# Layer-norm sums of the prompt in an mLSTM block: products with ones take the place of GpSimd's additions

## What is computed

```
def _head_layernorm(x, g):
    xf = x.astype(jnp.float32)
    xc = xf - jnp.mean(xf, axis=-1, keepdims=True)
    var = jnp.mean(xc * xc, axis=-1, keepdims=True)
    return xc * lax.rsqrt(var + EPS) * g.astype(jnp.float32)
...
# in _mlstm_chunked, for every frame of a chunk:
h = num / jnp.maximum(jnp.abs(den), jnp.exp(-mj))[..., None]
C_new = wpL[..., None, None] * C + jnp.einsum('bhs,bhsv,bhsd->bhvd', wsL, vb, kb)
...
hC = _head_layernorm(hC, p['mlstm_norm'][c]).reshape(B, T, C_INNER) + p['mlstm_skip'][c].astype(f32) * xc
```

## Time and profile before

| | |
|---|---|
| time, median of 3 runs | 2273.56 us (2268.47 to 2276.02) |
| time of the profiled execution | 2260.29 us |
| its span, first to last instruction | 2258.5 us |
| TensorE's mean granted clock | 0.965 of full |
| busy: PE, PEld | 2074.6 us (92%), 1879.0 us (83%) |
| busy: DVE, ACT, POOL | 863.3 us (38%), 429.3 us (19%), 919.6 us (41%) |
| the four loops over the units, together | 241.63 us |

### The profile page before, as it was taken

The page is one execution under the profiler, slowest core; times in us unless marked ns, Lnnn a source line. Parts: engine busy times, 40 slices in busy tenths (PEclk is TensorE's granted clock), DMA queues, the critical chain, the costliest instruction groups (busy, mean ns, idle before and its releaser), DMA issues.

```text
span 2258.5 us, 33584 instructions
## 1 busy us (share of the span) xinstructions
PE 2074.6 (92%) x13453; PEld 1879.0 (83%) x13453; DVE 863.3 (38%) x1115; ACT 429.3 (19%) x670; POOL 919.6 (41%) x584
## 2 busy tenths in 40 slices
PE   6999998889999999899999787878689899999997
PEld 5999987889999999899887263535389899999996
DVE  5654556442221012679322453544422322210125
ACT  3242333121110001222123131312100211100011
POOL 4333322354444444655442031313254544444443
PEclk9999999999999999999999998989789999999998
DMA  4121221112222222232222727272722122222222
GB/s 167 54 92 57 82 89 48 58 56 75 74 74 76 77 77 75 96 121 76 104 90 74 268 86 273 92 274 84 252 108 75 56 75 74 74 75 75 75 75 93
DMA packets 81879, 224.35 MB, mean 99 GB/s; under 512 B 6288, under 2 KB 11280, under 8 KB 81040
## 3 DMA queue, kind: packets, MB, share of 16 engines
q1 hardware_dynamic: 73152, 202.94, 26.5%
q10 hardware_dynamic: 8656, 20.39, 2.5%
HBM read 170.06 MB, written 53.25 MB: 99 GB/s over the span
## 4 chain that ended last, share of the span: by engine, by line
PE 75%; DVE 13%; DMA 5%; issue 3%; ACT 3%; DVEq 1%; SPq 0%; POOL 0%; ACTq 0%; POOLq 0%
PE psd L210 10%; PE psd L214 10%; PE psd L215 10%; PE psd L211 10%; PE psd L217 10%; PE psd L216 10%; DMA Cs<-st_c 4%; DVE cv L901 2%; DVE ntmp L284 2%; PE psm L389 2%; DVE Cs L1370 1%; PE psd L1207 1%; PE psd L1196 1%; PE psm L1298 1%; DVE cv L898 1%
## 5 line engine op out<-in xcount | busy, mean ns | idle before, releaser
L1810 POOL CAST whi<-wraw 128x1024 fp32r<-128x1024 f32 x224 | 236.4, 1055 | 915.4 <-PE psd L217 500.3
L1812 POOL TENSOR_TENSOR wlo<-wraw,whi 128x1024 fp32r<-128x1024 f32 x224 | 543.2, 2425 | 18.0
L210 PE MATMUL psd<-xh,whi 128*128 128x320 f32 x1280 | 405.8, 317 | 25.3 <-ACT xh L257 14.0
L214 PE MATMUL psd<-xl,whi 128*128 128x320 f32 x1280 | 401.3, 314 | 13.9 <-POOL xl L292 10.9
L216 PE MATMUL psd<-xh,wlo 128*128 128x320 f32 x1280 | 398.2, 311 | 0.0
L217 PE MATMUL psd<-xh,wlo 128*128 128x320 f32 x1280 | 398.1, 311 | 0.0
L215 PE MATMUL psd<-xl,whi 128*128 128x320 f32 x1280 | 398.0, 311 | 0.0
L211 PE MATMUL psd<-xh,whi 128*128 128x320 f32 x1280 | 397.9, 311 | 0.0
L210 PEld LDWEIGHTS psd<-xh,whi 128*128 128x128 f32 x1280 | 243.1, 190 | 29.8 <-issue 23.4
L214 PEld LDWEIGHTS psd<-xl,whi 128*128 128x128 f32 x1280 | 242.2, 189 | 21.9 <-POOL xl L292 15.8
L211 PEld LDWEIGHTS psd<-xh,whi 128*128 128x128 f32 x1280 | 243.0, 190 | 0.8 <-issue 0.2
(11 more groups left out here) (352 smaller groups left out, 2904.5 us busy)
## 6 DMA issues: line engine op xcount, KB each, us to landing
wraw<-w SPq DMA_DIRECT2D x224, 512.0 KB, 3.3
Cs<-st_c SPq DMA_DIRECT2D x32, 1024.0 KB, 8.1
c_s<-Cs SPq DMA_DIRECT2D x32, 1024.0 KB, 5.1
z_kept<-zb ACTq DMA_DIRECT2D x16, 320.0 KB, 2.2
ztp<-z_kept SPq DMA_DIRECT2D x4, 1024.0 KB, 7.7
c_p<-Cp SPq DMA_DIRECT2D x4, 1024.0 KB, 9.9
xT<-x SPq DMA_DIRECT2D x4, 640.0 KB, 6.7
x_kept<-xT ACTq DMA_DIRECT2D x1, 2560.0 KB, 8.6
```

Source lines behind the costliest of these rows:

```text
L210: pe.matmul(o0, wh, x0, start=st, stop=False)
L214: pe.matmul(o0, wh, l0, start=False, stop=False)
L1810: pool.tensor_copy(whi[s][:], wraw[s][:]).then_inc(w_high, 1)
L1812: pool.tensor_tensor(wlo[s][:], wraw[s][:], whi[s][:].bitcast(F32), ALU.subtract).then_inc(w_split, 1)
```

## The change

POOL's seven additions per head go, and with them the semaphore `G`. In unit 2 PE multiplies each of the four tiles of `hb` with `ones` and accumulates the products in `B[0]`; in unit 6 it does so with the four squares in `kT` and with `D` in `att`. The wait for `G` in unit 2 falls away, since the wait for `dn` already covers ACT's writing of `hb`; in unit 6 a wait for the last square takes the place of the waits for `sD` and for the last centred tile.

```diff
-                self.G = Steps(sem("m_G"), [("h", k) for k in range(1, KH)] + [("s", k) for k in range(1, KH)] + ["sD"])
...
                     if u == 2:
                         pe.wait_ge(S_.sem, S_.at("dn", h))
-                        pe.wait_ge(self.G.sem, self.G.at(("h", KH - 1), h))
-                        pe.matmul(B[0], ones, kT[:, 0, 0:SEQ], start=True, stop=True).then_inc(P_.sem, 1)
+                        for k in range(KH):
+                            mm = pe.matmul(B[0], ones, hb[:, KH * h + k, 0:SEQ], start=(k == 0), stop=(k == KH - 1))
+                        mm.then_inc(P_.sem, 1)
                     if u == 6:
-                        pe.wait_ge(self.G.sem, self.G.at("sD", h))
-                        pe.wait_ge(V_.sem, V_.at(("xc", KH - 1), h))
-                        pe.matmul(B[0], ones, kT[:, 0, 0:SEQ], start=True, stop=True).then_inc(P_.sem, 1)
+                        pe.wait_ge(S_.sem, S_.at(("sq", KH - 1), h))
+                        for k in range(KH):
+                            pe.matmul(B[0], ones, kT[:, k, 0:SEQ], start=(k == 0), stop=False)
+                        pe.matmul(B[0], ones, att[:, 0:SEQ], start=False, stop=True).then_inc(P_.sem, 1)
...
             def pool_head(self, pool, h):
...
-                one = kT[:, 0, 0:SEQ]
-                for k in range(1, KH):
-                    pool.wait_ge(S_.sem, S_.at(("num", k), h))
-                    if k > 1:
-                        pool.wait_ge(G_.sem, G_.at(("h", k - 1), h))
-                    pool.tensor_tensor(one, hb[:, KH * h, 0:SEQ] if k == 1 else one, hb[:, KH * h + k, 0:SEQ], ALU.add)\
-                        .then_inc(G_.sem, 1)
-                for k in range(1, KH):
-                    pool.wait_ge(S_.sem, S_.at(("sq", k), h))
-                    if k > 1:
-                        pool.wait_ge(G_.sem, G_.at(("s", k - 1), h))
-                    pool.tensor_tensor(one, one, kT[:, k, 0:SEQ], ALU.add).then_inc(G_.sem, 1)
-                pool.wait_ge(G_.sem, G_.at(("s", KH - 1), h))
-                pool.wait_ge(S_.sem, S_.at("D", h))
-                pool.tensor_tensor(one, one, att[:, 0:SEQ], ALU.add).then_inc(G_.sem, 1)
```

More of the change, by code:

```diff
@@ L1571, in pool_head @@
             def pool_head(self, pool, h):
-                S_, G_ = self.S, self.G
                 if h == 0:
```

## The result

The changed kernel takes 2291.02 us (median of 6 runs, 2286.74 to 2293.73), the kernel before 2273.76 us (median of 6, 2268.47 to 2276.55): 17.3 us more, ratio 1.0076 with a 95% interval of 1.0059 to 1.0094. The profiled execution took 2290.63 us. The forecast was 2289.0. Two executions further on, one of e4 and one of e12, took 2654 and 2632 us at a mean granted clock of 0.74, and the medians and ratios leave them out.

A forecast was written before the change was run, and what follows sets the result against it. PE's own work and the loads of the streams' memory, not POOL, were taken to bound the loops. Unit 6's 15.4 us plus 0 for unit 2 and 0 for waits, on 2273.6, gave 2289.0 us; range 2280 to 2298.

The forecast's parts named there:

- What bounds the kernel: In the loop over units, PE and loads of the streams' memory set the pace; POOL's sums were ready 10 and 17 us sooner.
- Unit 6, 15.4 us: Four more products per head on PE's own path in unit 6, nothing hiding them: 3.84 us per head, 15.4 over four.
- The price per product: Each added fp32 128x512 product with ones in units 2 and 6 takes 0.96 us on PE, 1.9 at the lower clock.
- Unit 2, 0 us: Three more products per head in unit 2, 2.9 us on PE, hidden by load waits: 0 us.
- The cover: Idle time ahead of unit 4, 7.66 us, hides unit 2's 2.9; unit 5's load keeps at least 0.6 us to spare.
- The clock: Rival: less low clock in the loops gives back nearly all, one in 25, or 3 to 8 us, one in 9.
- The rival's mechanism: The shorter wait ahead of unit 4, 4.8 us for 7.66, could keep the clock up: 1.8 us per head in three heads.
- The sum: Unit 6's 15.4 us, plus 0 for unit 2 and 0 for the waits, makes 15.4 us over the whole kernel.
- The three rivals outside of the range: Unit 2's products showing, 0.05; the clock giving all back, 0.04; POOL's additions having held something up, 0.02.
- The 4.8 us from the sum to the normaliser: Sign of being right: in unit 6, 4.8 us between the second sum's start and the start of `nu` in each head.
- a sign of being wrong: A head longer by over 5 us, with the wait for the load ahead of unit 5.
- The idle time ahead of unit 4: Sign of being right: PE's idle time there near 4.8 us where it was 7.66, with unit 4's start unchanged.

The follow-up runs named there:

- e4: Changed kernel with the variance's five products moved from unit 6 to the end of unit 5, ahead of the load wait: 2267.19 us, ratio 0.9973 to before.
- e12: Kernel before with variance and normaliser products moved to the end of unit 5, plus unread products at the end of unit 3: 2243.55 us, ratio 0.9864.
- e3: Kernel before with POOL's additions left out, each sum being one product over the first tile alone: 2270.92 us, ratio 0.9993.
- e2: Kernel before with only unit 6's sum made by five products, POOL still adding the four tiles for unit 2: 2287.09 us, ratio 1.0055.
- e10: Changed kernel with four unread products with ones added at the end of unit 5: 2280.74 us, ratio 1.0034 to before.
- e11: Kernel before with four unread products with ones added at the end of unit 5: 2262.59 us, ratio 0.9940.
- e1: Kernel before with only unit 2's sum made by four products, POOL still adding the squares and D: 2276.52 us, ratio 1.0010.
- e8: Changed kernel with unit 2's four products made twice over: 2279.86 us, ratio 1.0030 to before.
- e7: Changed kernel with unit 6's five products made twice over: 2303.41 us, ratio 1.0129 to before.
- e9: Changed kernel run and profiled once more, nothing altered: 2295.09 us, ratio 1.0082 to before.
- e0: Kernel before profiled once more, nothing altered: 2275.48 us.

## Why the prediction was right

- *What bounds the kernel.* Right: without POOL's additions and the waits for them the time is the same within 4 us (e3), and in the loops PE or the loads end last.
- *Unit 6, 15.4 us.* The place and the mechanism were right (e2, e4). The price per product was mis-sized: a row of products with the same ones matrix takes 4.40 us for five at full clock, not 4.80. In e10:

```profile
1400.83 3.70 PE L1281 MATMUL psd<-mqk,con 128*128 128x512 f32 x8
1404.37 1.02 PE L1282 MATMUL psd<-att,con 128*128 128x512 f32 x2
1405.23 0.38 PE L1285 MATMUL psm<-att,con 128*128 128x128 f32 x2
```

  Less the 0.96 of the one product before, this is 3.44 us per head, 13.8 in all where I had 15.4. Measured in the stretch: 12.3 us between e10 and e11, 11.6 between the changed kernel and the second profile of before.
- *Unit 2, 0 us.* The cover held for PE and for the load of unit 5: unit 4 starts 31.3 us behind unit 0 in the second head, as before. It was thinner than I worked out: unit 5's load took 11.3 us before, beside unit 4's load, and not the 7.37 to 9.46 that I compared with. In the changed kernel it took 8.7 us and landed 0.3 us ahead of its use. The whole part costs 0 to 5 us (e1), not the 0 that I took. The step that fell short is the first head: I asked only whether unit 3 would be late, and it is not, but the shorter idle time moves the low clock to unit 4, and unit 6 starts some 4 us later in five of six profiles. Why its load takes 9.9 us and not 7.3 stays open.
- *The clock.* The rival's mechanism exists, as e8 shows with twice the products, but three added ones don't reach it: over both profiles of the changed kernel unit 4's read went at the low clock in five of the six heads behind the first, and at full clock in one, after 4.22 us of idle time. The idle time of 3.72 us ahead of unit 6, after which the first profile went on at full clock, is no safe one: in the second profile of before the clock was down after 3.51 us in the first head and after 4.88 in the second. I took the first profile, 13 us below its median, as a picture of every execution. That this did no harm is luck: I had no reason to expect that both kernels lose about the same there. Of the change's 17.3 us the runs place some 12 in unit 6; the first head's unit 6 and the late load below are worth 2 to 5 us each where they come, and two profiles don't tell how often that is.
- *The sum.* 15.4 forecast, 17.3 measured (13.4 to 21.4 by the interval): a little too much for unit 6 and too little for unit 2, so that it came out this near is in part luck. The three rivals outside of the range had 0.11 between them and not the 0.15 that I wrote.
- *What I said the profile would show.* The 4.8 us from the sum to the normaliser were 5.37 in the second head, part of it at the low clock, and 4.40 with the clock up. The second head was longer by 9.1 us (118.3 for 109.2), which I had named as a sign of being wrong together with a wait ahead of unit 5; that wait is not there, and against the second profile of before the first three heads are longer by 6.0, 3.9 and 2.9 us. The idle time ahead of unit 4 is 4.89, as said.

## What to carry to other kernels

Ask of an added instruction where it stands against the next wait, not how busy its engine is: the same five products cost 14 us or more behind the wait for a load and nothing ahead of it. Look for work that can be moved from behind such a wait to ahead of it; here this was worth some 25 us (17 to 32 by the interval), more than anything that the change itself could bring. And where the granted clock in a stretch differs between executions of one kernel, take a second profile before a row of the first becomes a price.

## What the hardware showed that I had not expected

Useless products can shorten the time. With four of them in an idle time of 3.4 to 5.6 us PE's next unit runs at 2.4 GHz and not at 1.2 in seven of the eight heads of e10 and e11: 12.3 us less before, 14.3 after, by the medians. The Trainium skill ("TensorE: Matmul & The Clock Gate", HAM oscillation) describes the loss; the runs agree and give its size here.

The load for unit 2 comes late in one head of some executions. In five profiles (the changed kernel's two, e4, e8, e10) one head starts unit 2 at 15.2 to 15.6 us behind its unit 0, where the heads behind the first start it at 12.6 to 13.4 otherwise; in the changed kernel it is the third:

```profile
1485.19 1.94 PE L1195 MATMUL psd<-Cs,qz 128*32 128x512 f32 x8 [7.20 <-DMA Cs<-st_c]
```

The transfers of that stretch (1475 to 1486 us) hold a packet of the instruction queue. The two loads issued in it take 9.6 us in the mean, unit 2's own 9.9:

```profile
q1 hardware_dynamic: 1797, 3.58, 93.7%
q8 instruction: 1, 0.02, 0.8%
...
Cs<-st_c SPq DMA_DIRECT2D x2, 1024.0 KB, 9.6
```

The same stretch of before (1458 to 1467 us) has none, and unit 2's own load takes 7.7 us there:

```profile
q1 hardware_dynamic: 1450, 2.90, 95.4%
...
Cs<-st_c SPq DMA_DIRECT2D x2, 1024.0 KB, 8.2
```

All five late loads have such a packet 0.5 to 1.6 us behind their issue and take 9.9 to 10.2 us, where unit 2's load takes 7.2 to 8.0 us otherwise in the heads behind the first. The long load for unit 6 in the first head is of the same kind: 9.8 to 10.2 us in e1, e4, e7, e9 and e10 with a packet 0.6 to 1.5 us behind its issue, and 7.3 us without one in before, e0, e2 and e3. A packet 0.8 us ahead of the issue did no harm (7.8 and 7.4 us for unit 2's load in the second head of before and e0).

All these kernels have unit 2's four products, or eight, and none of the seven profiles with before's unit 2 has unit 2's load late; two others with four products (e1, e7) haven't either. But e11, with before's unit 2, has a long load too (9.6 us for unit 6 in the first head, with a packet 2.6 us behind its issue), so the added products are not what makes a load long. That they only shift where the packet falls, and that the packet lengthens the load, is argued from this coincidence, and not tried.
